# Expert blocks with 64-token and 96-token room in a two-layer encoder trunk, experts placed by load

## The reference, cut to what matters

```python
logits = (xt @ w_router).astype(F32)
top_val, top_idx = lax.top_k(logits, TOP_K)          # 2 of 8
top_w = jax.nn.softmax(top_val, axis=-1)
...
def swiglu(x, w_gate, w_up, w_down):                  # 1024 -> 2752 -> 1024
    return (jax.nn.silu(x @ w_gate) * (x @ w_up)) @ w_down
...
contrib = yp[dest] * w_s[:, None]
out = jnp.zeros((T, D)).at[tok_s].add(contrib)
```

## Time and profile before

| what | value |
|---|---|
| median of 3 runs | 1420.14 us (1419.03 to 1422.51) |
| profiled execution: own time | 1419.78 us |
| profiled execution: span from first to last instruction | 1417.9 us |
| PE busy | 97% of the span |
| DVE busy | 81% |
| ACT busy | 61% |
| stretch of the 8 expert blocks | from 660.4 us on, over half of the span |

### The profile page before, as it was taken

How to read it: one execution, slowest core, us unless ns; L and a number is a source line. 1 busy time by engine, 2 the same in 40 slices (tenths; PEclk the granted TensorE clock), 3 DMA queues, 4 the chain that set the end, 5 groups by cost and what they waited for, 6 DMA issues and landing times.

```text
span 1417.9 us, 18919 instructions
## 1 busy us (share of the span) xinstructions
PE 1376.2 (97%) x6511; PEld 1032.8 (73%) x6511; DVE 1150.8 (81%) x1202; ACT 866.8 (61%) x927; POOL 69.0 (5%) x62
## 2 busy tenths in 40 slices
PE   6999989999999999899999999999999999999998
PEld 3887768888887876677667776777767767777666
DVE  5989786645449888866989889889898898898988
ACT  4344636443335455536767777777777777776775
POOL 0020011000000110100210000000000000000300
PEclk9999999999999999999999999999999999999999
DMA  7443234965483344144999989989899899898996
GB/s 285 174 179 142 96 115 160 397 248 201 162 321 119 149 149 178 52 148 168 379 372 365 419 312 416 406 306 424 328 379 404 319 418 385 324 422 299 409 400 236
DMA packets 63302, 395.71 MB, mean 279 GB/s; under 512 B 7186, under 2 KB 7758, under 8 KB 23322
## 3 DMA queue, kind: packets, MB, share of 16 engines
q1 hardware_dynamic: 58282, 375.64, 68.4%
q10 hardware_dynamic: 3104, 12.58, 2.2%
q0 software_dynamic: 1872, 6.90, 1.5%
HBM read 376.22 MB, written 18.87 MB: 279 GB/s over the span
## 4 chain that ended last, share of the span: by engine, by line
PE 84%; DVE 9%; DMA 3%; ACT 2%; issue 2%; SPq 0%; POOL 0%; DVEq 0%; ACTq 0%
PE bank L1736 19%; PE bank L1460 19%; PE bank L1461 19%; PE bank L1712 12%; PE bank L1507 5%; DVE w_lo L972 4%; DMA raw<-in_moe 2%; PE bank L1502 2%; PE bank L1613 1%; PE bank L1473 1%; PE bank L1723 1%; DVE ys L961 1%; PE bank L1606 1%; ACT w_hi L661 1%; DVE tmp L961 1%
## 5 line engine op out<-in xcount | busy, mean ns | idle before, releaser
L972 DVE TENSOR_TENSOR w_lo<-raw,w_hi 128x2048 fp32r<-128x2048 f32 (+2 forms) x383 | 802.7, 2105 | 130.7 <-ACT w_hi L661 127.0
L661 ACT ACTIVATE w_hi<-raw 128x2048 fp32r<-128x2048 f32 (+2 forms) x383 | 675.0, 1767 | 166.6 <-PE bank L1736 70.1
L1460 PE MATMUL bank<-w_hi,hT_hi 128*96 128x512 f32 (+3 forms) x1232 | 487.6, 396 | 1.6 <-DVE hT_lo L961 0.9
L1461 PE MATMUL bank<-w_hi,hT_lo 128*96 128x512 f32 (+3 forms) x1232 | 477.6, 388 | 0.0
L1460 PEld LDWEIGHTS bank<-w_hi,hT_hi 128*96 128x96 f32 (+1 forms) x1232 | 213.2, 173 | 66.4 <-issue 3.2
L1461 PEld LDWEIGHTS bank<-w_hi,hT_lo 128*96 128x96 f32 (+1 forms) x1232 | 213.4, 173 | 59.9 <-issue 1.0
L1712 PE MATMUL bank<-w_lo,hT_hi 128*96 128x512 f32 (+3 forms) x880 | 232.9, 387 | 0.0
L1712 PEld LDWEIGHTS bank<-w_lo,hT_hi 128*96 128x96 f32 (+1 forms) x880 | 145.5, 167 | 52.5 <-DVE w_lo L972 2.9
L1736 PE MATMUL bank<-w_hi,act_lo 128*96 128x512 f32 (+3 forms) x440 | 119.6, 394 | 2.4 <-DVE act_lo L1299 2.4
L1736 PE MATMUL bank<-w_hi,act_hi 128*96 128x512 f32 (+3 forms) x440 | 119.8, 394 | 0.8 <-ACT act_hi L855 0.8
L1736 PE MATMUL bank<-w_lo,act_hi 128*96 128x512 f32 (+3 forms) x440 | 118.4, 391 | 0.0
(11 more groups left out here) (223 smaller groups left out, 1000.0 us busy)
## 6 DMA issues: line engine op xcount, KB each, us to landing
raw<-in_moe SPq DMA_DIRECT2D x224, 1024.0 KB, 9.0
raw<-in_mix SPq DMA_DIRECT2D x56, 1024.0 KB, 5.1
raw<-in_dense SPq DMA_DIRECT2D x28, 1024.0 KB, 4.9
raw<-in_moe SPq DMA_DIRECT2D x43, 512.0 KB, 3.5
raw<-in_moe SPq DMA_DIRECT2D x16, 768.0 KB, 7.5
slot_h<-x_squared ACTq DMA_DIRECT2D x1, 6144.0 KB, 45.5
slot_y<-x_squared ACTq DMA_DIRECT2D x1, 6144.0 KB, 18.6
slot_y<-y SPq DMA_DIRECT2D x8, 384.0 KB, 10.5
```

The lines of the kernel that those rows point to most:

```text
L661: nc.scalar.activation(HI[:, split_slot, 0:width], RAW[:, raw_slot, 0:width], ACT.Copy)\
L972: vec.tensor_tensor(LO[:, split_slot, 0:width], RAW[:, raw_slot, 0:width], HI[:, split_slot, 0:width].bitcast(F32), ALU.subtract).then_inc ...
L1460: mm(out_, left[0], right[0], start=start, stop=False)
L1461: mm(out_, left[1], right[1], start=False, stop=False)
```

## The change

The eight blocks now alternate. Blocks 0, 2, 4 and 6 are **light** (room for 64 tokens, `LCAP`), blocks 1, 3, 5 and 7 are **heavy** (96, the old `ffn_block`). Expert 0 stays in block 0. The other experts are ranked by their number of tokens: the four fullest go to the heavy blocks, the rest to the light ones (`router_blocks`); SP reads each block's expert from a table. Tokens beyond a block's room go to extra blocks as before.

In a light block the stationary operand has 128 columns: 64 tokens' high parts and the same tokens' low parts. One pass over the high weights and one over the low weights then give all products, the token's high sum in bank rows 0 to 63 and its low sum in rows 64 to 127. To add the two, ACT copies rows 64 to 127 to `LO_SUM` (`lo_copy`), and one matmul by a matrix that swaps the halves adds them to rows 0 to 63 (`add_lo`), before the silu. For the down product the halves are added once, in the next heavy block (`y_lo`, `add_y_lo`). Block 0 is written out apart and no longer waits for the number of blocks.

```diff
 CAP = 96
+LCAP = 64
+HEAVY = NE // 2
+PAIR = LCAP + CAP
 XTRA = (T * TOPK) // (CAP + 1)
 NBLK = NE + XTRA
-SLOT_ROWS = -(-(NBLK + 2) * CAP // P) * P
...
+    def router_blocks(dve, v, tt, ts, stt):
...
+        tt(key[:, :], total, key_row, ALU.add)
...
+        reduce(rank[:, :], cmp[:, 0, :, :])
+        v.settle()
+        ts(light[:, :], rank[:, :], float(HEAVY + 1), None, ALU.is_ge)
+        stt(start[:, :], rank[:, :], float(PAIR), start_row, ALU.mult, ALU.add)
+        stt(block_of[:, :], rank[:, :], 2.0, block_row, ALU.mult, ALU.add)
+        v.settle()
+        stt(room[:, :], light[:, :], float(LCAP - CAP), room_row, ALU.mult, ALU.add)
+        stt(start[:, :], light[:, :], float(CAP - HEAVY * PAIR), start[:, :], ALU.mult, ALU.add)
+        stt(block_of[:, :], light[:, :], float(1 - 2 * HEAVY), block_of[:, :], ALU.mult, ALU.add)
...
+                light_slabs(0, 0, slice(0, 1))
                 sp.wait_ge(sem("experts_known"), 1)
+                for i in range(HEAVY - 1):
+                    e = sp.value_load(R["nbe"][0:1, 2 * i + 1:2 * i + 2], min_val=0, max_val=NE - 1)
+                    heavy_slabs(2 * i + 1, i, bass.ds(e, 1))
+                    e = sp.value_load(R["nbe"][0:1, 2 * i + 2:2 * i + 3], min_val=0, max_val=NE - 1)
+                    light_slabs(2 * i + 2, i + 1, bass.ds(e, 1))
+                e = sp.value_load(R["nbe"][0:1, NE - 1:NE], min_val=0, max_val=NE - 1)
+                late_slabs(NE - 1, 0, bass.ds(e, 1))
...
+            def lo_copy(n, parity, width=CHUNK):
+
+                act.wait_ge(slab_used, n + 1)
+                nc.scalar.activation(LO_SUM[P - LCAP:P, 0:2 * width], PS[parity][P - LCAP:P, 0:2 * width], ACT.Copy)\
+                    .then_inc(sem("lo_copied"), 1)
+
+            def silu_light(q, k, parity, width=CHUNK):
+
+                act.wait_ge(sem("lo_added"), k + 1)
+                act.wait_ge(act_done, q)
+                nc.scalar.activation(R["silu"][0:LCAP, 0, 0:width], PS[parity][0:LCAP, 0:width], ACT.Silu).then_inc(silu_done, 1)
+
+            def turned_hi_light(q, parity):
+
+                act.wait_ge(turned, q + 1)
+                nc.scalar.activation(R["act_hi"][:, :, 0:LCAP], PS[2][:, 0:2 * CAP].rearrange("p (k t) -> p k t", k=2)[:, :, 0:LCAP], ACT.Copy)\
+                    .then_inc(act_hi_ready, 1)
...
+                def chunk(p, q, k, parity, n0, r0):
+
+                    turned_hi_light(q - 1, 1 - parity)
+                    ffn_split(p + 3, n0, r0)
+                    lo_copy(n0 + p + 1, parity)
+                    ffn_split(p + 4, n0, r0)
+                    silu_light(q, k, parity)
+                    ffn_split(p + 5, n0, r0)
...
+            def light_block(b):
...
+                def chunk(p, q, parity, n0):
+
+                    turned_lo_light(q - 1)
+                    ffn_split(p + 3, n0)
+                    ffn_split(p + 4, n0)
+                    mult_light(q, parity)
+                    ffn_split(p + 5, n0)
+
+                if fixed:
+                    chunk(4, qb + 1, 1, n0)
+                    router_blocks(dve, v, tt, ts, stt)
+                    chunk(7, qb + 2, 0, n0)
+                    router_places(dve, v, tt, ts, stt)
+                    chunk(4, qb + 3, 1, n0 + 6)
+                    scale_rows(0)
+                    chunk(7, qb + 4, 0, n0 + 6)
+                    scale_rows(1)
+                    chunk(4, qb + 5, 1, n0 + 12)
+                    router_rest(dve, v, tt, ts, stt)
+                    chunk(7, qb + 6, 0, n0 + 12)
+                    router_early(dve, v, tt, ts, stt)
+                    chunk(4, qb + 7, 1, n0 + 18)
+                    chunk(7, qb + 8, 0, n0 + 18)
...
+            def gate_up_light(n, s, k0, nk, width, parity):
+
+                pe.wait_ge(hi_ready, n + 1)
+                for k in range(nk):
+                    w_hi, _ = w_parts(s, k * 2 * width, (k + 1) * 2 * width)
+                    mm(PS[parity][:, 0:2 * width], HTH[:, k0 + k, 0:2 * LCAP], w_hi, start=k0 + k == 0, stop=False)
+                pe.wait_ge(lo_ready, n + 1)
+                for k in range(nk):
+                    _, w_lo = w_parts(s, k * 2 * width, (k + 1) * 2 * width)
+                    ins = mm(PS[parity][:, 0:2 * width], HTH[:, k0 + k, 0:2 * LCAP], w_lo, start=False, stop=k0 + k == KD - 1)
+                ins.then_inc(slab_used, 1)
+
+            def add_lo(k, parity, width=CHUNK):
+
+                pe.wait_ge(sem("lo_copied"), k + 1)
+                mm(PS[parity][:, 0:2 * width], R["swap"][:, :], LO_SUM[:, 0:2 * width],
+                   start=False, stop=True, skip_group_check=True).then_inc(sem("lo_added"), 1)
+
...
+                def pair(n0, qb, k0, start):
+
+                    for j in range(2):
+                        p, q = 4 + 3 * j, qb + 1 + j
+                        gate_up_light(n0 + p, slot(p), 0, 4, CHUNK, 1 - j)
+                        turn_act_light(q - 1)
+                        gate_up_light(n0 + p + 1, slot(p + 1), 4, 4, CHUNK, 1 - j)
+                        if start and j == 0:
+                            pe.wait_ge(y_taken, 2 * b + 2)
+                        down_light(n0 + p + 2, slot(p + 2), q - 1, start and j == 0)
+                        add_lo(k0 + 1 + j, 1 - j)
...
+            def add_y_lo(ready):
+
+                pe.wait_ge(sem("y_lo_ready"), ready)
+                for half in range(2):
+                    ins = mm(PS[4 + half][:, :], R["swap"][:, :], R["y_lo"][:, half * 512:half * 512 + 512],
+                             start=False, stop=True, skip_group_check=True)
+                ins.then_inc(sem("y_lo_added"), 1)
...
+                light_block(0, 0)
                 pe.wait_ge(sem("blocks_known"), 1)
                 nb = pe.value_load(R["nbi"][0:1, 0:1], min_val=NE, max_val=NBLK)
-                with pe.Fori(0, NE - 1) as b:
-                    ffn_block(b, True)
+                with pe.Fori(0, HEAVY - 1) as i:
+                    ffn_block(pe.snap(2 * i + 1), True, y_ready=2 * i + 2)
+                    light_block(pe.snap(2 * i + 2), pe.snap(i + 1))
                 with pe.Fori(NE - 1, nb) as b:
-                    ffn_block(b, True, True)
+                    ffn_block(b, True, True, 2 * HEAVY)```

What moves, at three places. On PE, a full chunk of an expert block: gate and up of its first slab, the turning over, gate and up of the second slab, down of the chunk before. Before, it is this (the second slab's gate and up repeats the first's, the last row is down):

```order
L1460 MATMUL bank<-w_hi,hT_hi 96x512
L1461 MATMUL bank<-w_hi,hT_lo 96x512
...
L1712 MATMUL bank<-w_lo,hT_hi 96x512 x4
...
L1723 MATMUL bank<-ident,act 128x96 x2
```

More of the change, by code:

```diff
@@ L389, in router, with reduce @@
         v.do(vec.tensor_copy(R["counts"][:, :], bank("pos", 0)[:, 0:(TB + 1) * NE]), *drain_of(1, "pos", 0))
+    def router_blocks(dve, v, tt, ts, stt):
+        vec = nc.vector
+        cmp, cmp2, nbf, over, cnt = (R[k] for k in ("cmp", "cmp2", "nbf", "over", "cnt"))
+        key, rank, light, start, block_of, room, excess = (R[k] for k in ("key", "load_rank", "light", "start", "block_of", "room", "excess"))
+        tril = R["moec"][:, MOEC_TRIL:MOEC_TRIL + 64].rearrange("p (a b) -> p a b", a=NE)
+        key_row, start_row, block_row, room_row = (R["moec"][:, at:at + NE] for at in (MOEC_KEY, MOEC_START, MOEC_BLOCK, MOEC_ROOM))
+        total = R["counts"][:, TB * NE:(TB + 1) * NE]
+        def reduce(dst, src):
+            v.do(vec.tensor_reduce(dst, src, AX_X, ALU.add))
@@ L404, in router_places @@
         vec = nc.vector
[L405 to L408, removed]
+        sel1, sel2, place, far = (R[k] for k in ("sel1", "sel2", "place", "far"))
+        cnt, jump, chosen, start, room = (R[k] for k in ("cnt", "jump", "chosen", "start", "room"))
         counted = R["counts"][:, 0:TB * NE].rearrange("p (t e) -> p t e", t=TB)
@@ L418, in reduce @@
             v.do(vec.tensor_reduce(dst, src, AX_X, ALU.add))
+        dve.wait_ge(sem("blocks_known"), 1)
+        tt(place[:, :, :], counted, per_token(start[:, :]), ALU.add)
+        tt(far[:, :, :], counted, per_token(room[:, :]), ALU.is_ge)
+        stt(jump[:, :], cnt[:, :], float(CAP), start[:, :], ALU.mult, ALU.subtract)
         v.settle()
[L421 to L428, removed]
+        stt(jump[:, :], jump[:, :], float(LATE_ROW + CAP), room[:, :], ALU.add, ALU.subtract)
         v.settle()
@@ L807, in _ @@
                 copy(R["sums"][:, :], R["moec"][:, 0:2 * P], sem("sums_ready"), 1)
+                for h in range(2):
+                    copy(R["swap"][:, h * LCAP:(h + 1) * LCAP], IDENT[:, (1 - h) * LCAP:(2 - h) * LCAP], sem("swap_ready"), h + 1)
             turned_h(0)
@@ L1365, in ffn_block @@
                 if is_moe:
-                    take_y(b)
+                    dve.wait_ge(sem("y_lo_added"), y_added)
+                    take_y(b, LCAP)
                 ffn_split(4, n0)
@@ new lines, in down_light @@
+            def down_light(n, s, q, start, stop=False, tiles=((0, P), (1, P))):
```

(17 more changed lines are left out.)

275 lines of the change are left out of this document (208 added, 67 removed).

## The result

| | before | after |
|---|---|---|
| median of 7 runs each | 1420.16 us (1418.89 to 1422.51) | 1426.84 us (1424.92 to 1431.9) |
| profiled span | 1417.9 us | 1424.6 us |
| PE busy | 97% | 92% |
| PE's mean granted clock | 0.995 | 0.982 |

A forecast was written before the change was run, and what follows sets the result against it. PE, busy 97%, was taken to set the pace. Light blocks -15.6, heavy blocks +2.8 and block 0 +5.5 sum to -7.3 us: 1419.8 to 1412.5, as a median 1413 us; range 1403 to 1425.

The forecast's parts named there:

- The light chunk, 7.55 us: Light blocks: a loop through PE, ACT and DVE sums to 7.51, taken as 7.55 us a chunk, 0.91 less than before.
- the loop is longer than I count: Rival, ACT and PE in every light chunk: hand-overs cost 0.2 more each, 8.5 us a chunk, 1439 us; chance 0.11.
- weight copy 1.79, `lo_copy` 0.48: ACT's two links in the light chunk's loop, in us, read from start distances of weight copies and of the y copy.
- Heavy blocks, +0.7 each: Heavy blocks: two `add_y_lo` matmuls (0.46) and a PE wait of about 0.2 for slab 4; +2.8 us in four blocks.
- Block 0, +5.5: Block 0: router rows on DVE delay the scatter, so slab 28 comes late and block 1 starts at 761.2 us.
- Landing: Block 0: the scatter lands 3.5 us after POOL's last issue at 727.0, releasing SP at 730.5; bounds 2.5 and 9.9.
- late-scatter rival: Rival, block 0: landing still takes 9.9 us, block 0 +11.9, total 1419 us; chance 0.14.
- The clock, 0.02: Rival, light chunks: PE idles 1.6 us in each and runs at half speed, time near 1520 us; chance 0.02.
- At nothing: the lead-in: Ahead of block 0: POOL's memsets and ACT's swap copies lie in idle time; PE starts block 0 about 0.7 us earlier.
- Transfers, 0.12: Rival, light chunks: stores and token loads slow the weight stream to 411 GB/s, 7.87 us a chunk, 1419 us; chance 0.12.
- The sign that was to tell them from the loop: Light blocks above 90 us: DMA share at 1.0 throughout would mean transfers, below 0.9 the loop.
- The weighed rule: HBM limit of about 358 GB/s a core: a block would need 96.6 us and the sum be +8; set aside.

The follow-up runs named there:

- e9: e7 with short useless matmuls keeping PE busy at its longest waits in the light blocks; 1419.9 us, ratio 0.9998 to the kernel before.
- e4: The changed kernel with short useless matmuls keeping PE busy at its longest waits in block 0; 1429.08 us, ratio 1.0058 to the kernel before.
- e11: e10 with block 0 in the light form again, kept busy by useless matmuls too; 1424.44 us, ratio 1.0026 to the kernel before.
- e1: The changed kernel with `lo_copy` behind both weight copies in light chunks and tail; 1428.76 us, ratio 1.0072 to the kernel before.
- e3: The changed kernel without the low-half copies and the matmuls adding them in gate and up (output incomplete); 1423.84 us, ratio 1.0017 to the kernel before.
- e10: e8 with short useless matmuls at its own longest PE waits in the light blocks; 1418.73 us, ratio 0.9986 to the kernel before.
- e5: The changed kernel loading only three quarters of each 1 MB expert slab (output wrong); 1426.72 us, ratio 1.0026 to the kernel before.
- e6: e5 with `lo_copy` behind both weight copies, and behind slab 4's copy at a light block's start; 1419.84 us, ratio 0.9982 to the kernel before.
- e12: e10 loading only three quarters of each 1 MB slab (output wrong); 1409.88 us, ratio 0.9942 to the kernel before.
- e7: The changed kernel with block 0 back in the 96-token form, `router_blocks` between its chunks; 1420.88 us, ratio 0.9998 to the kernel before.
- e8: e7 with the ACT order of e6 in the light blocks; 1425.3 us, ratio 1.0036 to the kernel before.

## Why the prediction was wrong, by its own steps

Span against span, forecast 1410.6 and measured 1424.6: 14.0 us. Of these 9.5 lie in light blocks 2, 4 and 6, 3.3 ahead of block 0 and 1.4 in it, and the heavy blocks take back 0.2.

*The light chunk, 7.55 us: right mechanism, term too small.* It took 7.82. The prediction named this loop, set the break-even at about 7.8, and gave the rival "the loop is longer than I count" 0.11. Per block: chunks +1.8, the tail 14.7 us for 14.1, the start 13.9 for 13.6, so 90.4 for 87.75 from PE's start. That is 8.0 us in three blocks, 5.3 of it in the chunks, the largest part of the miss. The failed step is "weight copy 1.79, `lo_copy` 0.48", which are 1.93 and 0.62: distances between starts of rows that overlap, put in for rows that do not.

*Light block 2*, 91.9 us: another 1.5, nearly all in its first chunk, 8.61 us for 7.3. With PE kept busy (e9) that chunk is 7.33, so it is the clock.

*Heavy blocks, +0.7 each: about right.* 94.0 us from PE's start in blocks 1, 3 and 5, +1.0; block 7 is 0.4 shorter.

*Block 0, +5.5: nearly the right sum by luck, from a wrong cause.* From PE's start it was to take 6.2 more and took 7.6. DVE's rows cost what was counted (3.4 for 3.5, 1.6 for 1.6, 1.2 a scaling). But two terms of the scatter failed. The second scaling ended at 716.95 instead of 709.5, which POOL made good with issues that took 9.1 us in all for 16.6, so that it ended at 726.3 as forecast. Landing was put at 3.5 us, "the queue has run empty"; it took 8.9, with SP issuing weight slabs up to 724.6 us, nearly the 9.9 of the late-scatter rival. SP passed the scatter at 735.29 instead of 730.5. Even so the wait for slab 28 did not take place, since DVE was later still. In its place stood the clock, which took some 4 us (43.9 for 48.1 in e4); e4 and e11 show that each of the two costs hides the other.

*The clock, 0.02: the largest misjudgement.* The rival was priced as one long fall to 1520 us and dismissed because PE had idled 5.3 of 40 us at 1.00. What mattered was short falls around single waits. The Trainium skill, "TensorE: Matmul & The Clock Gate", Why this matters for your kernels, warns of idle gaps between bursts of matmuls. The trace agrees in block 0: the clock fell to 0.50 during or within 1 us of waits of 3.58 and 3.51 us, and also 1.5 us behind one of 2.03.

*At nothing: the lead-in.* Block 0 began 2.6 us later instead of 0.7 earlier. The code ahead of it hardly differs, and in the twelve experiments, which share it, the y copy of block 0 lies anywhere from 663.7 to 671.8 us. The three at 671 and later (e1, e3, e10) ran from 654 to 668 us at a clock of 0.51, the change at 0.90. So this is no cost of the change that a single trace could show; how much of it is in the medians was not tried.

*Transfers, 0.12.* Wrong for the change (e5), right one step later (e3, e6, e12). The sign that was to tell them from the loop, a DMA share of 1.0 or below 0.9, could not: the share was 0.98 with the loop as the limit. The weighed rule was rightly set aside. The Trainium skill, "DMA: Bandwidth & Descriptors", Specifications, gives about 358 GB/s for a core; e10 moved 393 over a whole light block.

## What to carry to other kernels

When work is taken off the engine that sets the pace, add up the loop that remains, and where a link has no row of its own yet, give the sum with and without the overlap of the rows it is read from (here 7.5 and 7.8 us). Then count what the idle engine loses in clock. Put such a block where nobody else needs the slack: here block 0 carried 11.5 us of router rows; in the 96-token form it is only 1.7 us longer with them than in the kernel before, and giving it back that form undid the loss. If several limits lie within 3 us of each other, each repair only shows the next one.

## What the runs showed that I had not expected

A wait of PE of 1.4 to 4.7 us, at times with a shorter one beside it, can halve its clock for 3 to 17 us. It need not: waits of 1.73 and 1.77 us in block 0 of the change, and of 2.39 in e11, had no fall behind them. The fall may come later than the wait: in e6 PE waited up to 939.5 and again up to 944.2 us, ran at 1.00 between, and was at 0.50 from 946 to 952, without a gap:

```profile
942.00:944.00 2.00, 0.85 (x8) 0.45 (x6) 1.57 (x4) 1.99 (x5) 0.00 (x0) 1.00 0.86 237
944.00:946.00 2.00, 1.85 (x6) 1.30 (x7) 1.23 (x1) 0.87 (x2) 0.00 (x0) 0.86 1.01 350
946.00:948.00 2.00, 2.00 (x5) 1.06 (x5) 1.51 (x2) 1.16 (x3) 0.00 (x0) 0.50 0.96 370
```

Waits of about 1.1 us in every light chunk, with PE at work between them, did not lower it. Matmuls without use, put in the longest waits, kept the clock at 1.00 in all light blocks of e9 and e10, which were no longer for it than those of e7 and e8; across a wait of 4.72 us in e11 they did not.

The share of the DMA engines says little about bytes: in e10's last light block it is 1.01 at 424 GB/s and 1.02 at 329 near the block's end, where the smaller slabs go.

```profile
1250.00:1260.00 10.00, 9.03 (x38) 6.28 (x37) 9.62 (x7) 8.64 (x10) 0.00 (x0) 1.00 1.01 424
...
1302.00:1308.00 6.00, 5.09 (x27) 4.65 (x28) 4.83 (x6) 4.71 (x6) 0.00 (x0) 1.00 1.02 329
```
